# Spare transposes on TensorE, row squares on GpSimd and an earlier norm sum in a hybrid encoder step

## What is computed

```
x = x + 1/2 * SwiGLU_1(RMSNorm(x))
u = RMSNorm(x); P = u @ w_in
branch A: causal conv -> RG-LRU scan, times GeLU(gate); @ w_br_lru
branch B: causal conv, SiLU -> chunked SSD scan, gate, grouped RMSNorm; @ w_br_ssd
m = sigmoid(gA) * branchA + sigmoid(gB) * branchB
x = x + m @ w_out
x = x + 1/2 * SwiGLU_2(RMSNorm(x));  final RMSNorm
```

## Time and profile before

| what | value |
|---|---|
| median of 3 runs | 1859.58 us (1859.31 to 1860.30) |
| the profiled execution | 1859.9 us, span 1858.1 us |
| granted PE clock, mean | 0.997 |
| PE busy | 98% |
| DVE, ACT, POOL busy | 59%, 36%, 7% |
| DMA | 185 MB, mean 100 GB/s |

### The profile page before, as it was taken

One profiled execution on the slowest core, in us unless ns is written; L12 is line 12 of the kernel. 1 busy time (PEld: TensorE's weight loads), 2 busy tenths in 40 slices (PEclk: granted clock), 3 DMA queues, 4 the chain that ended last, 5 costly groups with the idle time before them and its releaser, 6 DMA issues.

```text
span 1858.1 us, 31082 instructions
## 1 busy us (share of the span) xinstructions
PE 1829.8 (98%) x12539; PEld 1780.3 (96%) x12539; DVE 1102.1 (59%) x1358; ACT 661.3 (36%) x878; POOL 125.6 (7%) x253
## 2 busy tenths in 40 slices
PE   8999999999989999999999999999999999999998
PEld 7999999999989999989989989998999999999998
DVE  6443343345787775787787877876755433442444
ACT  5221332123567752344244235233342211221224
POOL 3000000000011210111101101100200000000000
PEclk9999999999999999999999999999999999999999
DMA  5222222222422253363454335336622222222222
GB/s 149 68 79 68 79 75 72 79 68 70 137 63 75 68 148 101 113 178 86 120 147 120 108 94 168 108 108 214 194 68 79 79 68 80 74 73 79 68 68 91
DMA packets 273102, 185.09 MB, mean 100 GB/s; under 512 B 7340, under 2 KB 260468, under 8 KB 272768
## 3 DMA queue, kind: packets, MB, share of 16 engines
q1 hardware_dynamic: 239984, 129.52, 24.2%
q0 software_dynamic: 10240, 35.86, 6.2%
q10 hardware_dynamic: 22800, 18.62, 3.1%
HBM read 161.43 MB, written 22.53 MB: 99 GB/s over the span
## 4 chain that ended last, share of the span: by engine, by line
PE 89%; DVE 5%; ACT 2%; issue 2%; DMA 2%; ACTq 0%; DVEq 0%
PE pu L651 82%; DMA gbuf<-gate_spill 1%; PE pn L877 1%; PE pn L919 1%; PE pn L772 1%; PE pn L900 1%; PE pn L894 1%; DVE w_lo L1480 1%; PE pu L734 0%; PE pn L931 0%; ACT w_hi L1017 0%; PE pn L866 0%; DVE squares L1474 0%; PE pn L668 0%; PE pu L952 0%
## 5 line engine op out<-in xcount | busy, mean ns | idle before, releaser
L1480 DVE TENSOR_TENSOR w_lo<-w_raw,w_hi 128x1024 fp32r<-128x1024 f32 x240 | 294.0, 1225 | 460.2 <-ACT w_hi L1017 458.5
L651 PE MATMUL pu<-act_hi,w_hi 128*128 128x320 f32 x1940 | 453.0, 314 | 8.4 <-DVE xc L1474 2.2
L651 PE MATMUL pu<-act_lo,w_hi 128*128 128x320 f32 x1940 | 443.3, 309 | 1.1 <-DVE act_lo L1523 1.0
L651 PE MATMUL pu<-act_hi,w_lo 128*128 128x320 f32 x1940 | 442.8, 309 | 0.0
L1017 ACT ACTIVATE w_hi<-w_raw 128x1024 fp32r<-128x1024 f32 x240 | 253.6, 1056 | 511.2 <-PE pu L651 507.4
L651 PEld LDWEIGHTS pu<-act_hi,w_hi 128*128 128x128 f32 x1940 | 324.2, 188 | 25.4 <-issue 21.2
L651 PE MATMUL pu<-x_hi,w_hi 128*128 128x320 f32 x1440 | 328.9, 310 | 1.3 <-DVE ff_g L1536 1.3
L651 PE MATMUL pu<-x_lo,w_hi 128*128 128x320 f32 x1440 | 328.2, 309 | 0.0
L651 PE MATMUL pu<-x_hi,w_lo 128*128 128x320 f32 x1440 | 328.1, 309 | 0.0
L651 PEld LDWEIGHTS pu<-act_lo,w_hi 128*128 128x128 f32 x1940 | 325.3, 188 | 2.4 <-DVE act_lo L1523 1.5
L651 PEld LDWEIGHTS pu<-act_hi,w_lo 128*128 128x128 f32 x1940 | 325.2, 188 | 0.0
(11 more groups left out here) (334 smaller groups left out, 1870.4 us busy)
## 6 DMA issues: line engine op xcount, KB each, us to landing
w_raw<-in_ffn_w_up_dram SPq DMA_DIRECT2D x87, 512.0 KB, 3.8
w_raw<-in_w_in_dram SPq DMA_DIRECT2D x73, 512.0 KB, 3.9
w_raw<-in_ffn_w_down_dram SPq DMA_DIRECT2D x32, 512.0 KB, 3.6
da_rep<-e_spill POOLq DMA_DIRECT2D x20, 512.0 KB, 4.2
w_raw<-in_w_br_ssd_dram SPq DMA_DIRECT2D x16, 512.0 KB, 3.5
w_raw<-in_ffn_w_down_dram SPq DMA_DIRECT2D x16, 384.0 KB, 3.2
gate_spill<-gbuf ACTq DMA_DIRECT2D x18, 320.0 KB, 2.4
merged<-gate_spill POOLq DMA_DIRECT2D x8, 640.0 KB, 5.0
```

Source lines behind the costliest of these rows:

```text
L651: ins = pe.matmul(dst[:, h, :], w[:, side, c, :], a[:, k, h * HALF:(h + 1) * HALF], start=(at == 0), stop=(at == n - 1))
L1480: dve.tensor_tensor(w_lo[:, side, :, :], w_raw[:, side, :, :], w_hi[:, side, :, :].bitcast(F32), ALU.subtract).then_inc(s["w_lo_done"], 1)
```

## The change

- PE: five spare transposes of `ident` into `pn[0]` after the constants, eight more after the transpose of g1; five after feature tile 4 and five after tile 5 inside unit U_LRU + 1 of j = 0, and sixteen behind that unit. Nobody reads them.
- PE: the first norm sum stands ahead of unit 0 of the first FFN instead of behind it.
- POOL makes the row squares' diagonal tiles, one ahead of each of the first five vector DMAs; DVE no longer does.
- DVE copies the last x tile in two halves of four feature tiles. The first raises the new semaphore `x_half`, the second `out_free`. ACT waits for `x_half` ahead of x_hi tile 0 and for all copies only ahead of tile 4; its first weight quarter comes ahead of both waits.
- DVE writes `after` in `first_rows`, behind the first group of up units, instead of ahead of the FFN.
- DVE's `lru_split(j - 1)` stands behind g_t instead of ahead of t_r.

```diff
--- before.py
+++ after.py
@@ -141,7 +141,7 @@
 N_PARAMS, N_CONST = 25, 17
 
 
-SEMAPHORES = """const xin0 xin1 xin2 xin3 xin4 params w_in0 w_in1 w_hi_done w_lo_done out_ready out_free
+SEMAPHORES = """const x_half xin0 xin1 xin2 xin3 xin4 params w_in0 w_in1 w_hi_done w_lo_done out_ready out_free
 sq_clear sq_done sq_part sq_added sq_summed ln_ready rs_act rs_step xn_done xh_done xl_done raw_v ff_th ff_s ff_hi ff_lo start_v start_a g1_in w_part0 w_part1 w_part2 w_part_hi w_part_lo g1_mm g1_cp hist_mm vec_mm
 hist_in ext_in conv tail_in wg_in gates_mm lru_v lru_a htail_in spill e_out es_in0 es_in1 yl_hi_done yl_lo_done
 dt_v dt_a dt_p after_v da_in0 da_in1 xb_th xb_out z_th ssd_p ssd_a ssd_v bseq
@@ -477,7 +477,15 @@
                          (norm_mix_g, V_NMIX), (norm_ffn2_g, V_NF2), (ssd_norm_g, V_SNG), (b_gate, V_BG),
                          (norm_final_g.rearrange("(o d) -> o d", o=1), V_NFIN)):
                 rows.append((w[0].rearrange("(k p) -> k p", p=P), 1, c - 128))
-            for src, t, r in rows:
+            def row_squares(t):
+
+                pool.wait_ge(s["sq_done"], SQ_X + t + 1)
+                pool.tensor_tensor(rvar[:, t * P:(t + 1) * P], ident[:, :], xss[:, t:t + 1].to_broadcast([P, P]),
+                                   ALU.mult).then_inc(s["sq_added"], 1)
+
+            for n, (src, t, r) in enumerate(rows):
+                if n < NT:
+                    row_squares(n)
                 pool.dma_start(vec_rows[r:r + src.shape[0], t, :], src).then_inc(s["params"], 16)
             for c in range(STACK):
                 at = slice(c * DEC_B * HIST, (c + 1) * DEC_B * HIST)
@@ -751,9 +759,16 @@
                 n = DEC_B * KT
                 pe.transpose(pn[0][:, 1, 0:n], h0_rows[:, :], ident[0:n, 0:n]).then_inc(s["vec_mm"], 1)
 
+            def keep_busy(n):
+
+                for _ in range(n):
+                    pe.transpose(pn[0][:, 1, 0:P], ident[:, :], ident[:, :])
+
             pe.wait_ge(s["const"], 3)
+            keep_busy(5)
             pe.wait_ge(s["g1_in"], 16)
             pe.transpose(pn[1][:, 0, 0:KT], g1_rows[:, :], ident[0:KT, 0:KT]).then_inc(s["g1_mm"], 1)
+            keep_busy(8)
             for t in range(NT):
                 pe.wait_ge(s[f"xin{t}"], 16)
                 open_out(t)
@@ -761,7 +776,8 @@
                     ins = pe.transpose(pu[t % 2][:, k // 4, (k % 4) * P:(k % 4 + 1) * P],
                                        x_rows[:, t, k * P:(k + 1) * P], ident[:, :])
                 ins.then_inc(s["out_ready"], 1)
-            ffn(U_FFN1, O_FFN1, 0, x_hi, x_lo, act_hi, act_lo, XH_FFN1, lambda: norm_sum(SQ_X + NT), first_rows)
+            norm_sum(SQ_X + NT)
+            ffn(U_FFN1, O_FFN1, 0, x_hi, x_lo, act_hi, act_lo, XH_FFN1, lambda: None, first_rows)
 
 
             def lru_gates(j):
@@ -787,7 +803,9 @@
             for t in range(NT):
                 ins = pe.transpose(pn[1][:, 0, t * HEADS:(t + 1) * HEADS], dt_raw[:, t * P:(t + 1) * P], ident[0:HEADS, 0:HEADS])
             ins.then_inc(s["dt_p"], 1)
-            unit(U_LRU + 1, O_LRU + 1, 2, 2, 0, act_hi, act_lo, ready=("xh_done", "xl_done", XH_MIX, 0))
+            unit(U_LRU + 1, O_LRU + 1, 2, 2, 0, act_hi, act_lo, ready=("xh_done", "xl_done", XH_MIX, 0),
+                 amid={4: lambda: keep_busy(5), 5: lambda: keep_busy(5)})
+            keep_busy(16)
 
             def first_gates():
                 pe.wait_ge(s["dt_v"], 1)
@@ -1116,10 +1134,13 @@
                 act.activation(squares[:, :, 0:512], x_rows[:, t, :].rearrange("p (b c) -> p b c", b=2), ACT.Square,
                                accum_out=xss[:, t:t + 1]).then_inc(s["sq_done"], 1)
             act.wait_ge(s["g1_cp"], 1)
-            act.wait_ge(s["out_free"], NT)
             for k in range(KT):
                 if k % 2 == 0:
                     cut_part(k // 2)
+                if k == 0:
+                    act.wait_ge(s["x_half"], 1)
+                elif k == KT // 2:
+                    act.wait_ge(s["out_free"], NT)
                 act.activation(x_hi[:, k, :], resid[:, k, :], ACT.Copy, scale=g1[:, k:k + 1]).then_inc(s["xh_done"], 1)
             cut_weights(1, 2, 0)
 
@@ -1627,6 +1648,9 @@
 
             def first_rows():
 
+                dve.wait_ge(s["const"], N_CONST)
+                dve.tensor_tensor(after[:, :, :], le_mask[:, 0:1, :].to_broadcast([P, HPG, P]),
+                                  ident[:, :].unsqueeze(1).to_broadcast([P, HPG, P]), ALU.subtract).then_inc(s["after_v"], 1)
                 dve.wait_ge(s["hist_mm"], 1)
                 dve.tensor_copy(tail[:, :, HIST:TAIL].rearrange("p (b c) w -> p b c w", b=2),
                                 pn[1][:, :, 0:384].rearrange("p b (c w) -> p b c w", c=16))
@@ -1641,13 +1665,14 @@
             dve.wait_ge(s["g1_mm"], 1)
             dve.tensor_copy(g1[:, :], pn[1][:, 0, 0:KT]).then_inc(s["g1_cp"], 1)
             dve.wait_ge(s["const"], 2)
-            for t in range(NT):
+            for t in range(NT - 1):
                 dve.wait_ge(s["out_ready"], t + 1)
                 dve.tensor_copy(resid[:, :, t * P:(t + 1) * P].rearrange("p (b k) t -> p b k t", b=2),
                                 pu[t % 2][:, :, :].rearrange("p b (k t) -> p b k t", k=4)).then_inc(s["out_free"], 1)
-                dve.wait_ge(s["sq_done"], SQ_X + t + 1)
-                dve.tensor_scalar(rvar[:, t * P:(t + 1) * P], ident[:, :], xss[:, t:t + 1], None,
-                                  ALU.mult).then_inc(s["sq_added"], 1)
+            dve.wait_ge(s["out_ready"], NT)
+            for b in range(2):
+                dve.tensor_copy(resid[:, 4 * b:4 * b + 4, SEQ:TOK], pu[(NT - 1) % 2][:, b, :].rearrange("p (k t) -> p k t", k=4)).then_inc(
+                    s["out_free" if b else "x_half"], 1)
             dve.wait_ge(s["out_free"], NT)
             for k in range(KT):
                 if k % 2 == 0:
@@ -1660,9 +1685,6 @@
                 stt(x_lo[:, k, :], resid[:, k, :], g1[:, k:k + 1], x_hi[:, k, :].bitcast(F32),
                     ALU.mult, ALU.subtract).then_inc(s["xl_done"], 1)
             cut_weights(1, 2, 0)
-            dve.wait_ge(s["const"], N_CONST)
-            dve.tensor_tensor(after[:, :, :], le_mask[:, 0:1, :].to_broadcast([P, HPG, P]),
-                              ident[:, :].unsqueeze(1).to_broadcast([P, HPG, P]), ALU.subtract).then_inc(s["after_v"], 1)
             ffn(U_FFN1, O_FFN1, 0, 0, act_hi, act_lo, False)
 
             norm_scale(1, 1.0 / D_MODEL, between=lambda: cut_weights(U_DT + 2, 1, 0))
@@ -1720,14 +1742,14 @@
                 done(dve.tensor_scalar(g_q[:, :], g_2[:, :], GELU_A, 1.0, ALU.mult, ALU.add))
                 lv(LV_P)
                 done(dve.tensor_tensor(halves(g_q[:, :]), halves(g_q[:, :]), out(O_LRU + r), ALU.mult))
-                if not first:
-                    lru_split(j - 1)
                 la(LA_TI)
                 done(dve.tensor_scalar(t_r[:, :], t_r[:, :], 1.0, lru_c[:, bass.ds(j, 1)], ALU.add, ALU.mult))
                 done(stt(t_i[:, :], t_i[:, :], 1.0, xc[:, :], ALU.add, ALU.mult))
                 la(LA_TG)
 
                 stt(halves(g_t[:, :]), halves(g_t[:, :]), 1.0, out(O_LRU + r), ALU.add, ALU.mult).then_inc(s["out_free"], 1)
+                if not first:
+                    lru_split(j - 1)
                 la(LA_A2)
 
                 done(stt(l_t2[:, :], l_a2[:, :], 1.0, l_t2[:, :], ALU.add, ALU.mult))
```

## The result

The changed kernel took 1850.2 us (median of 5 runs, 1849.62 to 1850.85) against 1860.3 (1859.31 to 1862.21) for the kernel before, measured together: a ratio of 0.9945, 95% interval 0.9933 to 0.9956. It gained 10.1 us where 8.0 were forecast. Its profiled execution took 1850.2 with a span of 1848.3, so 9.8 us are to be found between the two spans.

The account below looks back on a forecast made before the run. PE, busy 98% of the span, was taken as the bound, losing time to waits and lower-clock stretches. Head 3.8, g_t 2.95 and loop 1.2 sum to 7.95, say 8: 1859.58 becomes 1851.6, range 1849.8 to 1855.2.

Parts of the forecast that it names:

- forecast A: Whole kernel: the expected course, 1851.6 us, own range 1850 to 1853.3; chance 0.60.
- Norm sum ahead, ff_g off the path: First FFN: norm sum falls into PE's idle time, ff_g no longer holds PE, third unit at 28.95 instead of 32.77.
- Head, 3.8: Start to third unit: earlier fills, copies and norm sum start that unit 3.8 us earlier; first copy near 6.4.
- POOL's squares, 0.35: Head: each row square takes POOL 0.35 us, POOL keeps up, and square 4 is done near 11.6.
- rival B: Head: POOL becomes the wait at 1.21 us a square; head gain 2.2, total 1853.3; chance 0.12.
- Behind g_t, 2.95: Mixer near 545 us: moving lru_split removes PE's 1.53 us wait and the clock's fall; net gain 2.95 us.
- Loop, 1.2: Loop j = 4 to 7: the same order saves 0.3 us in each of four passes, 1.2 us.
- Mixer's spare transposes, gain 0: Mixer's head: they fit PE's waits, cost 0 (up to 1 us at the lower clock) and by themselves gain 0.
- Rival C: After 546 us or elsewhere: one or two clock falls remain or appear, 1.8 us each; 1853.4 to 1855.2; chance 0.16.
- Rival E: SSD groups: shifted sampling makes gaps trip the clock, 1.8 us each; seven falls, 1864, decides from five; chance 0.04.
- Rival D: Head and mixer: fills do not raise the clock, head gain about 1 us, total 1854.5; chance 0.04.
- Rival F: Mixer: PE was not held by g_t, so only the head gains; 1855.5; chance 0.04.

Follow-up runs that it names:

- double_sixteen: The changed kernel with thirty-two instead of sixteen spare transposes behind unit U_LRU + 1; 1851.2 us, ratio 0.9948.
- no_fills: The changed kernel without any of the 39 spare transposes; 1854.01 us, ratio 0.9964.
- split_only: The kernel before with one edit, DVE's lru_split behind g_t; 1856.56 us, ratio 0.9982.
- head_only: The changed kernel without the mixer's spare transposes and with lru_split in its old place; 1855.22 us, ratio 0.9973.
- no_mixer_fills: The changed kernel without the twenty-six spare transposes of the mixer's head; 1851.36 us, ratio 0.9952.

## Why the prediction was right, and where its sizes were off

The forecast was 1851.6 with a range of 1849.8 to 1855.2; 1850.2 lies in it, and the trace shows forecast A's course up to the SSD groups. By its steps:

- **Norm sum ahead, ff_g off the path: right.** Third unit behind unit 1 without a gap (22.68 + 7.30, then 29.99). With the sum back behind unit 0 the chain to ff_g holds PE again until 31.82. That no fall near 15.7 would come held too.
- **Head, 3.8: measured 2.8.** The step that failed is the first. "They cost 0.13 us" and "the upper level from tile 1 on": g1's transpose ran at 3.25 and not at 3.00, the eight from 3.45, and the first matmul of tile 0, landed at 4.60, stands at 5.21, 0.5 later than before. The sixteen loads of tiles 0 and 1 stand 0.21 apart (5.00 to 8.20), and only those of tile 2, from 8.63, 0.11 apart: the first record of the upper level is at 8.47, where it was 8.82 before. So the first copy came at 7.24 and not 6.4, later even than the 6.82 of the kernel before. "The loads do not hold it" failed too, by less: tile 4 landed at 11.22 (9.99 in the first profile), 0.1 behind the moment that its buffer came free (copy from 9.89, 1.22 long). In double_sixteen, with the same head, it landed at 10.23 and the third unit starts at 29.80, so late loads are some 0.2 of the miss. From the last copy on the sums hold: w_lo at 13.69 instead of 12.7, cut of unit 1 done at 22.64 (8.95 behind it; 9.25 forecast), third unit at 29.99 instead of 28.95 (its predecessor took 7.30, not 7.04). The error of 1.0 at w_lo is the error of the head.
- **POOL's squares, 0.35: measured 0.40**; the last is done at 12.85, not 11.6, since it waits for ACT and ACT for tile 4. POOL keeps up, and rival B is out. PE waits 0.57 for the last one, where with DVE it waits 1.76; but DVE's cut for unit 1 sets the path, and by the third unit the move is worth 0.2 us, 0.4 against double_sixteen.
- **The Trainium skill, SBUF — State Buffer, "Who interferes with whom"**, was cited for the low end: a DVE instruction with at most one SBUF input, outside the 2-port modes, does not contend with GpSimd. The first square, at 6.78 with no copy running, took 0.40 us and the four beside copies out of PSUM 0.40 to 0.43, which agrees with it; the 1.21 of the row did not come.
- **Behind g_t, 2.95: measured 2.9** (PE is 2.78 earlier at the first gates, 5.67 at those of j = 2). g_t starts at 541.68 and no stop over 0.2 us is left. The fall went with it. **Loop, 1.2: measured 1.2**, passes of 16.24.
- **Mixer's spare transposes, gain 0: mis-sized.** They cost nothing, as forecast (sixteen fit the gap; 32 do not). But the step "no fall of the clock is seen right there now" took one profile for all. Of the seven profiles without them four show a fall between 514 and 524 us, of the seven with them none; if the four fell by chance on any of the 14, all would be among those seven in 35 of 1001 cases. By the medians they bring about 1.2 us. Rival C happened in this form: not in the changed kernel, but in kernels that lack one of its parts, and in a part of their profiles.
- **SSD groups, 0: measured 3.0.** This was in no term and in no rival. Rival E looked at these groups for falls of the clock; there were none. The gain is that of the code load, which every kernel with at least thirteen transposes more has, whichever they are. It is also some 2 us of the 3.8 that no_fills lost. Without it the change would have been worth 7, one below the forecast. So the total came near by luck, through two misses of opposite sign (head -1.0, SSD +3.0).
- **Rival D, fills count for nothing:** PE did nothing but transposes before 8.47, the record there shows the upper level, and its next loads stand 0.11 apart. Before the unit for xc sixteen transposes stand where PE stood still for 2.2 us, and no fall followed in seven profiles. The Trainium skill, TensorE: Matmul & The Clock Gate, "Part 4: PE-mode transpose", says that transposes do not count as activity; these runs go against that rule. The thirteen ahead of the first tile are no evidence for either side, since no earlier rise from them shows in the time.
- **Rival F** is out: with `lru_split` moved alone the stop is gone and 3.7 us with it.

Three slips of arithmetic in the rivals carry nothing: POOL's row in B ends at 15.5 by its own terms and not at 15.3; F, the head alone, is 1859.6 - 3.8 = 1855.8; and in E five falls at 1.8 each only take back the gain (1860.6), so it would decide from seven on.

The parts do not add up as the terms did. split_only (3.7) and head_only (5.1) make 8.8, but head_only has the 2 to 3 us of the code load in it and keeps two falls; no_mixer_fills, with both parts and the moved load, makes 8.1; the mixer's transposes bring it to about 10.

## What to carry to other kernels

Where PE stands still for some microseconds for a thing that can't come sooner, spare transposes that fit the gap can keep its clock at the upper level (no fall there in seven profiles, four falls in the seven without). They must end before the awaited piece arrives: sixteen did, thirty-two made the next unit 1.07 us late, and thirteen ahead of the first tile delayed it by 0.5. Put a step whose result PE's buffers wait for ahead of one that nobody is waiting for: that alone gave 3.7 us here. And before an edit's gain is put down to its mechanism, run an edit of the same length that does nothing: thirteen instructions too small to matter brought 2.8 us (0.9 to 4.3 by the interval) where the whole change brought 10.1.

## What the runs showed of the hardware that was not expected

- A load of program code (one packet of 16 KB, 0.95 to 1.86 us long at this place in the 14 profiles) can hold back the last sixteenth of another queue's transfer: a 256 KB write took 3.64 to 4.51 us instead of 2.2. Whether it does depends on where in time the load falls, and that moves by 3 us with thirteen instructions more on PE.
- The clock's fall is not a property of the kernel alone. Of five profiles with the same stop of 1.5 us near 546, three show a fall behind it (548.13, 547.74, 545.68) and two none. The spread of times is wider too where stops are left, 1852.88 to 1857.32 for head_only, which keeps two, against 1849.62 to 1850.85 for the changed kernel; that the falls make this spread is not shown.
- PE's first rise to the upper level, with tiles of x coming in, is recorded at 8.47 us when PE has been at transposes since 1.99, and at 7.96 when it has only been since 4.64. In the 14 profiles it lies between 6.38 and 10.38, and what sets it was not settled.
